# Softmax division moved into the turning of the probabilities: a matmul with a diagonal matrix in place of scaling and transpose

## What is computed

```python
def row_step(args):
    q_r, r = args
    ...
    s_loc = jnp.where(valid, s_loc + bias[None], NEG_INF)      # local keys
    s_ctx = jnp.einsum('bhnqd,bhcd->bhnqc', q_r, kcx) * scale  # 256 context keys
    s = jnp.concatenate([s_loc.reshape(B, H, n_cb, NA_COL_BLOCK, n_loc), s_ctx], axis=-1)
    p = jax.nn.softmax(s, axis=-1)
    ...
    return (jnp.einsum('bhnqrk,bhrnkd->bhnqd', p_loc, v_blk)
            + jnp.einsum('bhnqc,bhcd->bhnqd', p_ctx, vcx))
```

## Time and profile before

| | us |
|---|---|
| median of 3 executions | 1697.31 |
| lowest and highest | 1691.6, 1702.64 |
| the profiled execution, its own time | 1694.15 |
| its span in the trace | 1692.4 |
| PE busy | 1496.7 (88%) |
| DVE busy | 720.4 (43%) |
| ACT busy | 546.1 (32%) |
| POOL busy | 662.8 (39%) |

### The profile page before, as it was taken

The page is one execution under the profiler, slowest core; times in us unless marked ns, Lnnn a source line. Parts: engine busy times, 40 slices in busy tenths (PEclk is TensorE's granted clock), DMA queues, the critical chain, the costliest instruction groups (busy, mean ns, idle before and its releaser), DMA issues.

```text
span 1692.4 us, 21447 instructions
## 1 busy us (share of the span) xinstructions
PE 1496.7 (88%) x7921; PEld 1164.7 (69%) x7921; DVE 720.4 (43%) x975; ACT 546.1 (32%) x818; POOL 662.8 (39%) x324
## 2 busy tenths in 40 slices
PE   5897999997848478998997899999999999999995
PEld 1237788775625357776785788887887788887883
DVE  5232422347645257785378831112335521111225
ACT  3432222163321146676343222222222232222221
POOL 1016555433300045441734344444555354444440
PEclk9999999998968788999997999999999999999996
DMA  8544433321285533444333233332333433333331
GB/s 302 163 140 132 121 109 100 103 65 51 92 188 116 101 88 107 116 127 147 101 88 100 75 90 96 99 97 86 98 94 96 125 99 95 91 98 93 91 101 50
DMA packets 283541, 183.37 MB, mean 108 GB/s; under 512 B 11810, under 2 KB 272688, under 8 KB 282841
## 3 DMA queue, kind: packets, MB, share of 16 engines
q1 hardware_dynamic: 280035, 170.33, 35.5%
q10 hardware_dynamic: 3446, 12.24, 2.2%
HBM read 165.73 MB, written 8.81 MB: 103 GB/s over the span
## 4 chain that ended last, share of the span: by engine, by line
PE 69%; DVE 13%; ACT 5%; DMA 4%; POOL 4%; issue 2%; SPq 1%; ACTq 1%; DVEq 0%; POOLq 0%
PE ps L1503 35%; PE ps L1508 18%; DMA zt<-zs 2%; PE ps L1543 2%; PE ps L1797 2%; PE ps L1554 1%; PE ps L1774 1%; PE ps L1763 1%; POOL w_lo L891 1%; DVE a_f L1401 1%; POOL hb_lo L911 1%; DVE x L1402 1%; PE ps L1700 1%; SPq L481 1%; DVE a_f L1367 1%
## 5 line engine op out<-in xcount | busy, mean ns | idle before, releaser
L891 POOL TENSOR_TENSOR w_lo<-raw,w_hi 128x1024 fp32r<-128x1024 f32 x206 | 511.8, 2487 | 638.2 <-ACT w_hi L572 638.1
L1503 PE MATMUL ps<-hb_hi,w_hi 128*128 128x512 f32 (+1 forms) x1264 | 493.7, 392 | 40.9 <-ACT w_hi L572 15.0
L1503 PE MATMUL ps<-hb_lo,w_hi 128*128 128x512 f32 (+1 forms) x1264 | 488.0, 388 | 0.0
L572 ACT ACTIVATE w_hi<-raw 128x1024 fp32r<-128x1024 f32 x206 | 216.6, 1053 | 305.1 <-PE ps L1508 260.4
L1508 PE MATMUL ps<-hb_hi,w_lo 128*128 128x512 f32 (+1 forms) x1264 | 308.7, 387 | 6.1 <-POOL w_lo L891 6.0
L1503 PEld LDWEIGHTS ps<-hb_hi,w_hi 128*128 128x128 f32 x1264 | 243.0, 192 | 96.4 <-issue 22.3
L1503 PEld LDWEIGHTS ps<-hb_lo,w_hi 128*128 128x128 f32 x1264 | 243.1, 192 | 47.0 <-issue 1.0
L1508 PEld LDWEIGHTS ps<-hb_hi,w_lo 128*128 128x128 f32 x1264 | 234.3, 190 | 56.1 <-POOL w_lo L891 8.0
L1503 PE MATMUL ps<-a_hi,w_hi 128*128 128x512 f32 x352 | 137.2, 390 | 4.8 <-ACT w_hi L572 4.8
L1503 PE MATMUL ps<-a_lo,w_hi 128*128 128x512 f32 x352 | 137.0, 389 | 0.0
L859 ACT ACTIVATE a_hi<-a_f 128x512 f32 (+1 forms) x44 | 27.8, 632 | 218.2 <-DVEq L1431 218.2
(11 more groups left out here) (232 smaller groups left out, 1741.5 us busy)
## 6 DMA issues: line engine op xcount, KB each, us to landing
raw<-in_ffn_w_gu SPq DMA_DIRECT2D x88, 512.0 KB, 3.8
raw<-in_w_in SPq DMA_DIRECT2D x54, 512.0 KB, 3.9
ada1x<-in_ada_w SPq DMA_DIRECT2D x32, 512.0 KB, 4.0
raw<-in_ffn_w_down SPq DMA_DIRECT2D x32, 512.0 KB, 3.9
ada<-in_ada_w SPq DMA_DIRECT2D x4, 2048.0 KB, 17.7
kspec<-spec SPq DMA_DIRECT2D x8, 1024.0 KB, 17.0
raw<-in_w_out SPq DMA_DIRECT2D x16, 512.0 KB, 4.0
raw<-in_ffn_w_down SPq DMA_DIRECT2D x16, 384.0 KB, 3.3
```

Of the source, the lines that this page charges most:

```text
L572: act.activation(w_hi[:, b, :], raw[:, b, :], ACT.Copy).then_inc(hi_done, 1)
L891: pool.tensor_tensor(w_lo[:, b, :], raw[:, b, :], w_hi[:, b, :].bitcast(F32), ALU.subtract).then_inc(lo_done, 1)
L1503: pe.matmul(dst, w_hi[:, b, k * P:(k + 1) * P], x, start=start and k == 0 and n == 0, stop=False)
```

## The change

The scaling of `pr` is taken out. In its place DVE multiplies the 128x128 identity by the same `arec` into a new tile `scale_d` (two buffers by unit parity, two heads), which is then a diagonal matrix with one over the sum of each query. PE turns the unscaled `pr` by an ordinary float32 matmul with `scale_d` as the moving operand instead of a transpose with `ident`. The semaphores and the order of the instructions stay.

```diff
+        scale_d = at("scale_d", P_HY + 18432, [2, 2, P])
...
                         link(dve.reciprocal(arec[:, n % 2, e:e + 1], asum[:, n % 2, e:e + 1]))
-                        dve.tensor_scalar(pr[:, n % 2, e, 0:L + CTX], pr[:, n % 2, e, 0:L + CTX], arec[:, n % 2, e:e + 1], None, ALU.mult).then_inc(nrm_ok, 1)
+                        dve.tensor_scalar(scale_d[:, n % 2, e, :], ident[:], arec[:, n % 2, e:e + 1], None, ALU.mult).then_inc(nrm_ok, 1)
...
                     for c, (a, m) in enumerate(chunks[0:4]):
-                        pe.transpose(ps[0:m, 4 + e, c * P:(c + 1) * P], pr[:, b, e, a:a + m], ident[:])
+                        pe.matmul(ps[0:m, 4 + e, c * P:(c + 1) * P], pr[:, b, e, a:a + m], scale_d[:, b, e, :], start=True, stop=True)
...
                 for e in range(2):
-                    ins = pe.transpose(ps[:, 6, e * P:(e + 1) * P], pr[:, b, e, a:a + m], ident[:])
+                    ins = pe.matmul(ps[:, 6, e * P:(e + 1) * P], pr[:, b, e, a:a + m], scale_d[:, b, e, :], start=True, stop=True)
```

## The result

| | before | changed |
|---|---|---|
| median, us | 1696.71 (4 runs) | 1722.3 (4 runs, 1720.88 to 1723.81) |
| ratio | 1 | 1.015, 95% interval 1.0115 to 1.0184 |
| span of the profiled execution, us | 1692.4 | 1720.8 |
| attention: first `scores` to first matmul of the output projection, us (PE stands idle for the last 5.8 to 5.9 of them, before and after) | 166.1 (633.55 to 799.69) | 189.5 (633.53 to 823.07) |
| what follows it, us | 892.7 | 897.8 |

A second set of runs of the changed kernel gave 1722.92 (1.0168, 1.012 to 1.0216). The change makes the kernel 1.5% slower.

The account below looks back on a forecast made before the run. The prediction took PE to bound the attention. PE's added 34.6 us and 1.1 at the start, less 10.6 for stalls and clock, 1.5 for DMA waits and 0.5 at the end, made +23.1: 1719 us, range 1711 to 1727.

Parts of the forecast that it names:

- What bounds: In most attention blocks PE sets the pace, busy all 4.41 us; DVE has about 1 us to spare.
- DVE's saving: The 64 scalings, 57 us on DVE, become 128 columns wide, below 0.3 us each; 35 to 40 us go.
- Two records: In the turn, an ordinary float32 matmul takes two records where a transpose takes one: 512 and 128 records.
- The size of a record: A 128-column record on PE takes 0.108 us, scaled from 256 and 512 columns; 320 matmuls add 34.6 us.
- The stalls: PE's waits for DVE's scaling at blocks 4, 12 and 20 shrink from about 1.8 to 0.3 us; relief 10.6 us.
- PE's lateness: PE reaches the second head 2.6 us later, its inputs only 1.08 us later, so each stall shrinks by 1.5 us.
- The clock: PE's clock holds at blocks 4, 12 and 20; at two of them this saves 3.07 us each.
- The smaller terms: Waits for the DMA of `ada1` vanish, -1.5 us; attention's end, -0.5; its first turn at half clock, +1.1.
- (c): Rival, chance 0.03: in the turn a matmul costs four times a transpose, +105 us less the relief, about 1787.
- (b): Rival, chance 0.05: in the turn a full-width record costs 62.5 ns, not 108, so not slower: 1688.
- (a): Rival, chance 0.17: the clock still falls at the two stall places, or at others: +31 us, 1727.
- (d): Rival, chance 0.05: the short scaling gets behind POOL's work anew, stalls don't shrink at three places: +38 us, 1734.

Follow-up runs that it names:

- float32r run: The changed kernel with the turn's two operands, exponentials and diagonal matrices, rounded to float32r, one record per chunk: 1694.63 us, ratio 0.9989.
- the matmul half alone: Kernel before with the turns as ordinary float32 matmuls with the identity, DVE still scaling all 544 or 640 columns: 1724.39 us, ratio 1.0176.
- the DVE half alone: Kernel before with DVE writing the 128-column diagonal matrices, turns still transposes with the identity, probabilities left undivided: 1689.22 us, ratio 0.996.
- both kernels with POOL in pieces: Kernel before with POOL's L937 and L939 cut into pieces: 1682.02 us; the same with L937 whole for the first pair of heads: 1685.57 us.

## Why the prediction was right, and where its terms were off

- **What bounds.** Right: PE sets the pace in all but the few blocks named, and DVE's 15 us fewer of scaling show up in the others as nothing (an undisturbed block takes 4.40 us with the short instruction alone, as before). DVE's saving itself was put too high: 57 us of scalings became 42, not 20. Beside an idle POOL the short instruction takes 0.29 us, as forecast; but 35 of the 64 run beside a POOL instruction, and those hold 34 of the 42 us.
- **Two records.** Right: 512 and 128 records. The float32r run shows that the second record is the whole price.
- **The size of a record.** The term "320 x 0.108 = 34.6 us" was too small: it measured 38.7. Within the turn, 1.98 us for 16 records against 1.02 for 8, so a chunk costs 0.12 us more and not 0.108. The two column counts it was scaled from, at 256 and 512, gave no fixed part; at 128 columns the step is about 0.112 us, and the first step of a group, which I counted as before, takes longer as well (0.213 us against 0.165): two chunks alone cost 0.55 - 0.27 = 0.28 us more.
- **The stalls.** The relief was forecast as 10.6 us and measured as about 12.2 (blocks 4 and 12 with the block behind each: 13.74 to 11.0 although 2.4 of PE work were added, 5.1 each; block 20: 10.67 to 11.0, 2.0). The mechanism, PE's lateness, was right: the matmul half alone gives 11.0 of it. But it is not the only way to that relief, as the prediction had it: the DVE half alone gives 7.3 in its profile, 6.1 of them by the clock. PE came later by 1.21 a block, and the stalls went to 0.25 us with the long scaling and to about 0.1 with the short one, not to 0.3. The statement that the short instruction would be held as the long one was right too (2.77 us).
- **The clock.** It held in the attention from the start to the last 2 to 5 us, as forecast, in every profile in which all turns, or those of one head, were ordinary float32 matmuls. The Trainium skill (TensorE: Matmul & The Clock Gate, PE-mode transpose) would say so for the reason that transposes don't count as work for the clock. No run here shows that reason: with transposes kept the clock held as well (the DVE half alone, and both kernels with POOL in pieces), and with float32r matmuls it fell once.
- **The smaller terms.** DMA waits: 5.54 and 4.84 us to 5.63 each, and 0.1 us at block 25: 1.7 us absorbed against 1.5. The end: 0.4 against 0.5. The start was forecast at +1.1 and came out at -1.0 in the first profile, where full clock came back in the middle of the first turn (its eight chunks took 2.96 us; a later turn takes 2.05); in the second profile of the changed kernel the eight took 3.58 us, all at half clock, and the start came out at about 0.
- **Against the rivals.** The factor 4 (c) fell, and with it the +105 us worked out from it: a chunk went from 0.13 to 0.25 us, a factor of 2. The cheap record (b) fell with it. The falls of clock (a) and new waits behind POOL (d) did not come.

The mechanism held and the sum came out at +23.1 us against +23.4 in the attention and +25.6 in the medians. That it is so close is partly luck: PE's price was 4.1 us too low, what the waits, the start and the end give back 3.8 us too low (11.5 against 15.3), and the two offset one another.

## What to carry to other kernels

Folding a scale into a float32 transpose is not free: the matmul that takes its place takes twice the PE time, so it pays only where PE has room for it, and here PE was the engine without any. Look first at what makes the long instructions of the other engine long: here DVE's scalings were held by POOL, and cutting POOL's low parts (one instruction into five, two into two each, for each pair of heads) gave 0.7%, without changing what is computed. And a stall of the pacing engine shrinks by itself when work is added ahead of it, so price an addition as work minus waits.

## What the runs showed of the hardware beyond the expected

- DVE's scaling of 128 columns takes 0.29 us when POOL is idle and up to 2.77 us beside POOL. Nearly all scalings beside POOL ended shortly after one POOL instruction did (0.08 to 0.38 us, by their columns), also where POOL had the next one ready; cutting POOL's instruction let DVE finish 0.30 us after the first piece at all three places (0.79 us in all). But at one other place DVE stayed out for 3.67 us while POOL ran several instructions without a pause. What decides between the two is open.
- PE idle for 1.3 to 1.8 us in all within a block was followed by a half-clock stretch in some places and not in others; some 1.8 us at blocks 4 and 12 of the kernel before was followed by one, at block 20 it was not, and with float32r 1.6 us at block 20 was and at block 12 was not.
- With the same instructions in it, the part behind the attention varies by up to 9.6 us between profiles (892.3 to 901.9). A change of half a per cent is read from its own stretch of the trace, and its worth from many runs.
